# Finishing a job's tokens inside the expert loop of a two-layer transformer kernel, instead of in a pass of its own at the end

## The reference, cut to what matters

```python
def moe_swiglu(t, w_router, w1, w3, w2):          # t: (2048, 1024)
    logits = (t @ w_router).astype(jnp.float32)
    top_v, top_i = lax.top_k(logits, TOP_K)        # 2 of 8 experts
    gates = jax.nn.softmax(top_v, axis=-1).astype(t.dtype)
    e_flat = top_i.reshape(-1)
    order = jnp.argsort(e_flat)
    tok = order // TOP_K
    xs = t[tok]
    sizes = jnp.bincount(e_flat, length=N_EXPERTS).astype(jnp.int32)
    h = jax.nn.silu(lax.ragged_dot(xs, w1, sizes)) * lax.ragged_dot(xs, w3, sizes)
    y = lax.ragged_dot(h, w2, sizes) * gates.reshape(-1)[order][:, None]
    return jnp.zeros_like(t).at[tok].add(y)

# end of the layer: x = x + ga_f * rmsnorm(moe_swiglu(hx), g_ffn_post)
```

## Time and profile before

| | us |
|---|---|
| median of 3 runs | 8557.16 (8553.48 to 8563.33) |
| profiled execution, its own time | 8556.28 |
| its span | 8554.4 |
| TensorE busy | 8155.5 (95%) |
| GpSimd busy | 4284.0 (50%) |
| VectorE busy | 4087.5 (48%) |
| ScalarE busy | 1476.7 (17%) |

### The profile page before, as it was taken

One profiled execution on the slowest core, in us unless ns is written; L12 is line 12 of the kernel. 1 busy time (PEld: TensorE's weight loads), 2 busy tenths in 40 slices (PEclk: granted clock), 3 DMA queues, 4 the chain that ended last, 5 costly groups with the idle time before them and its releaser, 6 DMA issues. The chain is left out here.

```text
span 8554.4 us, 124971 instructions
## 1 busy us (share of the span) xinstructions
PE 8155.5 (95%) x43578; PEld 6035.7 (71%) x43578; DVE 4087.5 (48%) x8920; ACT 1476.7 (17%) x3720; POOL 4284.0 (50%) x4061
## 2 busy tenths in 40 slices
PE   8987999899999999897999999999999999999995
PEld 5575666547777777545777777777777777777774
DVE  3345455334444545644545554455455444444444
ACT  1134323221010101132222111111011011010001
POOL 0010667605656565314666665665665554654433
PEclk9999999999999999998999999999999999999997
DMA  6443788834444443225666666665665555554435
GB/s 262 158 142 121 261 300 298 304 113 170 153 153 158 162 153 106 91 95 183 220 225 228 219 212 214 208 208 196 211 204 194 195 193 177 194 184 161 155 127 199
DMA packets 781420, 1604.46 MB, mean 188 GB/s; under 512 B 47229, under 2 KB 556077, under 8 KB 734465
## 3 DMA queue, kind: packets, MB, share of 16 engines
q1 hardware_dynamic: 735686, 1451.02, 48.3%
q0 software_dynamic: 45280, 147.42, 5.5%
HBM read 1292.61 MB, written 304.71 MB: 187 GB/s over the span
## 5 line engine op out<-in xcount | busy, mean ns | idle before, releaser
L3211 PE MATMUL ex_ps<-ex_xt,ex_w 128*128 x6272 | 956.7, 296 | 31.4 <-issue 31.4
L3211 PEld LDWEIGHTS ex_ps<-ex_xt,ex_w 128*128 128x128 f32 x6272 | 861.3, 191 | 139.7 <-issue 139.7
L3211 PE MATMUL ex_ps<-ex_tx,ex_w 128*128 x6272 | 942.8, 293 | 14.8 <-DVE ex_tmp L3469 14.8
L3522 DVE TENSOR_TENSOR ex_ym<-ex_ps,ex_ym 128x512 f32<-128x512 f32 x1176 | 811.2, 690 | 238.9 <-PE ex_ps L3267 238.8
L3211 PE MATMUL ex_ps<-ex_tx,ex_sm 128*128 x6272 | 887.5, 295 | 15.3 <-issue 12.7
L3211 PEld LDWEIGHTS ex_ps<-ex_tx,ex_w 128*128 128x128 f32 x6272 | 857.5, 191 | 22.9 <-DVE ex_tmp L3469 20.2
L3072 POOL TENSOR_TENSOR ex_sa<-ex_a 128x128 f32<-128x128 f32 x182 | 82.7, 455 | 1561.8 <-DVE ex_a L3461 1561.8
L3211 PEld LDWEIGHTS ex_ps<-ex_tx,ex_sm 128*128 128x128 f32 x6272 | 847.4, 194 | 16.2 <-issue 16.1
L3057 POOL TENSOR_TENSOR ex_sm<-ex_w 128x512 f32<-128x512 f32 x394 | 507.6, 1288 | 119.5 <-DMA ex_w<-in_o_w 74.2
L3329 ACT ACTIVATE ex_tmp<-ex_ps 128x144 f32<-128x144 f32 (+4 forms) x392 | 116.3, 297 | 2350.9 <-PE ex_ps L3211 2350.1
L3063 POOL TENSOR_TENSOR ex_sm<-ex_w,ex_sm 128x512 f32<-128x512 f32 x394 | 501.6, 1273 | 30.9
(11 more groups left out here) (480 smaller groups left out, 14293.2 us busy)
## 6 DMA issues: line engine op xcount, KB each, us to landing
ex_w<-in_o_w SPq DMA_DIRECT2D x593, 1024.0 KB, 5.0
ex_wt<-wt SPq DMA_DIRECT2D x197, 1024.0 KB, 7.0
ma_cqT<-in_o_w SPq DMA_DIRECT2D x112, 1024.0 KB, 7.2
wt<-ma_bt SPq DMA_DIRECT2D x112, 1024.0 KB, 5.1
de_wr<-in_e_w SPq DMA_DIRECT2D x88, 1024.0 KB, 5.3
xs<-de_zero POOLq DMA_DIRECT2D x136, 512.0 KB, 4.8
en_ch<-in_w_mod SPq DMA_DIRECT2D x48, 1024.0 KB, 5.5
de_w<-in_e_w SPq DMA_DIRECT2D x44, 1024.0 KB, 7.3
```

The costliest lines, as they stand in the source:

```text
L3211: last = nc.tensor.matmul(PS[:, bank, 0:h], left[:, k], right[k], start=start and k == 0, stop=k == HK - 1, skip_group_check=not start)
L3522: nc.vector.tensor_tensor(out, new, out, ALU.add).then_inc(y_added[t], 1)
```

## The change

- `finish` handles 4 tiles (512 table rows, those of the last job) instead of 16. It gathers `z` and `x` by GpSimd (8 indirect DMAs) through an index array `LAST`, and each scatter to `out` waits for the one before.
- While a job runs, the tokens of the job before are finished: 4 tiles of 128 rows, in two buffers `Z`. GpSimd gathers the `z` rows after steps 0 (tiles 0, 1), 6 and 7. ScalarE squares and sums them and takes the roots (`roots`, after chunks 1 and 8), followed by a small Silu (`warm`); VectorE inverts (`invert`, after chunks 2 and 9); ScalarE scales (`norms`, after chunks 3 and 10); GpSimd multiplies by the gate's row and issues a gather of `x` that adds into the tile (`scale`, after steps 4, 5, 11, 12), and scatters to `out` (`store`, after steps 5, 6, 12 and ahead of step 13). A token is stored once for each of its two jobs, and the later store is the whole one.
- ScalarE's loop over chunks 0 to 9 becomes a loop over 0, 1, then chunks 2, 3, a loop over 4 to 8, and chunk 9.
- SyncE no longer waits for `stored` at a job's front; the loads of `IX` are issued between chunk 10's and chunk 11's weight loads. `y_free` is gone: VectorE and GpSimd wait for `stored` themselves. At the job's end SyncE waits for the stores to `out` and loads `LAST`.

The diff, cut to its core:

```diff
-def finish(nc, z_d, x_d, order_d, gate, out):
-    DEPTH = 8
+def finish(nc, z_d, x_d, LAST, gate, out):
+    TILES = LAST.shape[1]
...
         @block.gpsimd
         def _(pool):
-            pool.wait_ge(const_in, 32)
-            for t in range(NT):
+            for t in range(TILES):
+                pool.indirect_dma_start(out=Z[:, t], out_offset=None, in_=z_d, ...).then_inc(z_in[t], 16)
+            for t in range(TILES):
+                pool.indirect_dma_start(out=X[:, t], out_offset=None, in_=x_d, ...).then_inc(x_in[t], 16)
+            for t in range(TILES):
                 pool.wait_ge(summed, t + 1)
+                if t:
+                    pool.wait_ge(stored, 16 * t)
                 pool.indirect_dma_start(out=out, ...)
...
@@ SyncE in experts
                     load_low(e, 1, 1)
-                    row = listed(sp, 0, j, ROWS_END)
-                    sp.wait_ge(stored, j * 64 + 64)
-                    sp.sem_inc(y_free, 1)
+                    sp.wait_ge(tr_done, j * (2 * TILES) + 2 * TILES)
+                    load_x(sp.snap((j + 1).with_bounds(min_val=1, max_val=JOBS)))
+                    replace(0, 0, e, 2, None, None)
+                    with sp.Fori(0, (FC - 4) // 2) as q: ...
+                    sp.wait_ge(stored, j * 64 + 64)
+                    row = listed(sp, 0, j, ROWS_END)
...
                     sp.wait_ge(y_added[t], i * job + (job + 1))
+                    sp.wait_ge(o_stored[0], j * 32 + 32)
+                    sp.wait_ge(o_stored[1], j * 32 + 32)
+                    sp.dma_start(LAST[:, :, :], names(0, BANK)[:, 14:16].rearrange("(t p) w -> p t w", p=P)).then_inc(last_in, 16)
@@ GpSimd in experts
+            def gather(j, tile):
+                s = tile % 2
+                if tile == 0:
+                    pool.wait_ge(last_in, j * 16 + 16)
+                    pool.wait_ge(stored, j * 64 + 64)
+                if tile >= 2:
+                    pool.wait_ge(o_stored[s], j * 32 + 16)
+                pool.indirect_dma_start(out=Z[:, s], out_offset=None, in_=z_d, ...).then_inc(z_in[s], 16)
+            def scale(j, tile):
+                s = tile % 2
+                pool.wait_ge(normed, j * 4 + (tile + 1))
+                nc.gpsimd.tensor_tensor(Z[:, s], Z[:, s], G[:, :], ALU.mult).then_inc(scaled, 1)
+                pool.wait_ge(scaled, j * 4 + (tile + 1))
+                pool.indirect_dma_start(out=Z[:, s], out_offset=None, in_=x_d, ..., compute_op=ALU.add).then_inc(x_added[s], 16)
+            def store(j, tile):
+                s = tile % 2
+                pool.wait_ge(x_added[s], j * 32 + 16 * (tile // 2 + 1))
+                if tile:
+                    pool.wait_ge(o_stored[1 - s], j * 32 + 16 * ((tile - 1) // 2 + 1))
+                pool.indirect_dma_start(out=out, ..., in_=Z[:, s], in_offset=None).then_inc(o_stored[s], 16)
...
                     for f in range(FC):
+                        if f == FC - 1:
+                            store(j, 3)
                         step(f, 1 - f % 2, j * (FC // 2) + (f + 1) // 2)
+                        if f == 0:
+                            gather(j, 0)
+                            gather(j, 1)
+                        if f in (4, 5, FC - 3, FC - 2):
+                            scale(j, {4: 0, 5: 1, FC - 3: 2, FC - 2: 3}[f])
+                        if f in (5, 6, FC - 2):
+                            store(j, {5: 0, 6: 1, FC - 2: 2}[f])
+                        if f in (6, 7):
+                            gather(j, f - 4)
                         if f == FC - 2:
                             gather_gates(j, h)
                     add_rows(i, j, t, h)
@@ ScalarE in experts
+                    def roots(pair):
+                        for s in range(2):
+                            tile = 2 * pair + s
+                            act.wait_ge(z_in[s], j * 32 + 16 * (pair + 1))
+                            nc.scalar.activation(XT[:, bass.ds(other, 1), HK:HK + 2, :]..., Z[:, s], ACT.Square,
+                                                 accum_out=ss[:, 0, tile:tile + 1]).then_inc(squared, 1)
+                        nc.scalar.activation(ss[:, 1, 2 * pair:2 * pair + 2], ss[:, 0, 2 * pair:2 * pair + 2], ACT.Sqrt, ...).then_inc(rooted, 1)
+                        nc.scalar.activation(warm[:, :], eps[:, :], ACT.Silu)
+                    def norms(pair):
+                        act.wait_ge(inverted, j * 2 + (pair + 1))
+                        for s in range(2):
+                            nc.scalar.activation(Z[:, s], Z[:, s], ACT.Copy, scale=ss[:, 2, 2 * pair + s:2 * pair + s + 1]).then_inc(normed, 1)
-                    with act.Fori(0, FC - 4) as f:
+                    with act.Fori(0, 2) as f:
                         chunk(f)
+                    roots(0)
+                    chunk(2)
+                    chunk(3)
+                    norms(0)
+                    with act.Fori(4, 9) as f:
+                        chunk(f)
+                    roots(1)
+                    chunk(9)
                     for f in range(FC - 4, FC):
                         chunk(f, TURNS.get(f, ()))
+                        if f == FC - 4:
+                            norms(1)
@@ VectorE in experts
-                            dve.wait_ge(y_free, j + 2)
+                            dve.wait_ge(stored, j * 64 + 64)
...
-                    chunk(0)
-                    chunk(1)
-                    with dve.Fori(2, FC - 4) as f:
+                    for f in range(3):
                         chunk(f)
+                    invert(0)
+                    with dve.Fori(3, 9) as f:
+                        chunk(f)
+                    chunk(9)
+                    invert(1)
```

More of the change, by code:

```diff
@@ L2834, in _ @@
             act.wait_ge(eps_set, 1)
-            for t in range(NT):
-                act.wait_ge(z_in[t % DEPTH], 16 * (t // DEPTH + 1))
+            for t in range(TILES):
+                act.wait_ge(z_in[t], 16)
                 if t:
                     act.wait_ge(squared, t)
-                nc.scalar.activation(junk[:, :], Z[:, t % DEPTH], ACT.Square, accum_out=stat[:, 0, t:t + 1]).then_inc(squared, 1)
+                nc.scalar.activation(junk[:, :], Z[:, t], ACT.Square, accum_out=stat[:, 0, t:t + 1]).then_inc(squared, 1)
                 act.wait_ge(squared, t + 1)
@@ L2845, in _ @@
             nc.vector.memset(eps[:, :], EPS).then_inc(eps_set, 1)
-            dve.wait_ge(const_in, 32)
-            for t in range(NT):
-                s = t % DEPTH
+            dve.wait_ge(const_in, 16)
+            for t in range(TILES):
                 dve.wait_ge(rooted, t + 1)
@@ L2851, in _, with experts @@
                 dve.wait_ge(inverted, t + 1)
[L2852 removed]
+                nc.vector.scalar_tensor_tensor(Z[:, t], Z[:, t], stat[:, 2, t:t + 1], G[:, :], ALU.mult, ALU.mult).then_inc(scaled, 1)
                 dve.wait_ge(scaled, t + 1)
[L2854 to L2858 removed]
+                dve.wait_ge(x_in[t], 16)
+                nc.vector.tensor_tensor(X[:, t], X[:, t], Z[:, t], ALU.add).then_inc(summed, 1)
+def experts(nc, xs_d, cols, ident_d, w1, w3, w2, wt, CT, GG, tab_d, no_share_d, share_d, z_d, x_d, gate, out, LAST):
     F = w1.shape[2]
@@ L2972, in _ @@
                     load_low(e, 0, 0)
+            sp.dma_start(G[:, :], gate.rearrange("(a n) -> a n", a=1).to_broadcast([P, D])).then_inc(g_in, 16)
+            sp.dma_start(LAST[:, :, :], table[ROWS_END:ROWS_END + BANK, 14:16].rearrange("(t p) w -> p t w", p=P)).then_inc(last_in, 16)
             sp.dma_start(share_d[SEQ:SEQ + BANK], no_share_d).then_inc(shares_in, 16)
@@ L3023, in _ @@
                         sp.sem_inc(ix_in, 16 * (7 - small))
-                    sp.wait_ge(tr_done, j * (2 * TILES) + 2 * TILES)
-                    sp.sem_inc(passed_sp, 1)
-                    load_x(sp.snap((j + 1).with_bounds(min_val=1, max_val=JOBS)))
-                    replace(0, 0, e, 2, None, None)
-                    with sp.Fori(0, (FC - 4) // 2) as q:
-                        for s in range(2):
-                            f = q * 2 + (s + 1)
-                            replace(f, 1 - s, e, at(f + 2), e, at(f + 1))
                     replace(FC - 3, 1, e, FC - 1, e, FC - 2)
@@ L3045, in _ @@
             sp.wait_ge(sums["s4"], (n + ahead) * (2 * FC) + 2)
+            sp.sem_inc(passed_sp, 1)
+            sp.wait_ge(last_in, (n + ahead) * 16 + 16)
             sp.sem_inc(passed_sp, 1)
@@ L3145, in _ @@
             weight_sums(1, 0, 1, 0)
+            pool.wait_ge(g_in, 16)
             for t, h in enumerate(HALVES):
@@ L3568, in build @@
         POS = m.sbuf("pos", [P, 2, NT], U32)
+        LAST = m.sbuf("last", [P, BANK // P, 2], U32)
         CT, GG = m.sbuf("ct", [1, 4, LIST], I32), m.sbuf("gg", [P, 3, NT])
@@ L3577, in build @@
                     a["blank"], a["names"], table, POS, CT, RI, GG, ident)
-        experts(nc, xs, cols[1, 1, :, 0], ident, a["o_w1"], a["o_w3"], a["o_w2"], wt, CT, GG, table, a["no_share"], share, z)
```

(3 more changed lines are left out.)

95 lines of the change are left out of this document (62 added, 33 removed).

## The result

The changed kernel takes 8628.45 us (median of 4 runs, 8625.57 to 8630.5) beside 8557.08 us before: ratio 1.0082, 95% interval 1.0071 to 1.0094. It is slower by 71 us where 19 were forecast, and the time lies above the range.

The account below looks back on a forecast made before the run. GpSimd was taken to set the time at job fronts, TensorE in the expert stage, with DMA work bare in `finish`. 58 + 12 + 7 - 39 - 19 = +19 gave 8576 us, 8-in-10 range 8540 to 8612.

Parts of the forecast that it names:

- Costed at nothing: Expert stage: other steps' GpSimd work (at most 5.8 us) fits its idle time ahead of `left_sums`, 8.6 us in the mean chunk.
- Finish: Tail after the experts: fewer tiles end it at 8515 instead of 8554.4 us, gain 39 us, between 31 and 46.
- The bounds for a store's landing: In `finish`: each of four successive stores takes between 3.95 and 7.65 us; 5.5 was taken.
- the stretch before it: From the last L3136 to the barrier ahead of `finish`: claimed to stay as it was.
- Table loads: ScalarE, h = 128 jobs: only the loop over chunks 0 and 1 still reloads for `keep`; gain 19 us.
- Fronts and clock: Job fronts: GpSimd's added `scale` and `store` delay TensorE, 58 us; seven new gaps lower its clock, 12 us.
- Norms: ScalarE, second pair's `norms` between `take` and `keep`: `keep` 2.0 us late, costing TensorE 7 us in all.
- Rival 1: Job fronts: GpSimd's new work does not reach TensorE, so the 58 and 12 us vanish, 8506 us; chance 12%.
- Rival 2: GpSimd waits for landings at 11 fronts, 22 us, and `roots` for `z` in h = 128 jobs, 8; 8601 us; 20%.
- Rival 3: ScalarE's table loads stay where they are, so 19 us of gain are missing, 8595 us; chance 10%.
- VectorE's inversions, SyncE's move and the DMA traffic: Expert stage: two inversions, earlier loads at the front and some 6 MB more DMA in a job, all put at no cost.

## Why the prediction was wrong

The sign was right, and the size was 52 us short. The step that failed is in **Costed at nothing**: "The other steps' GpSimd work [...] lies in GpSimd's idle time ahead of `left_sums`". The cover was taken as a mean over all chunks, and only GpSimd's own lateness was asked about. The work behind step 11 does lie in that idle time (7.12 us of it are left in the rows above), and still it costs 39.5 us: it holds VectorE, whose token sums of chunks 12 and 13 run beside it, and TensorE waits for VectorE. The work behind step 12 was costed, but for its delay of GpSimd at the front alone; it holds VectorE's token sums of chunk 13 too, another 15.2 us. Together they are the +54.7 us of the table above. This is shown by the product and its gather moved one chunk on their own (-37 us), the product and the adding gather left out one at a time (23.2 and 32.3 us left), the lone product at two places (14 and 0 us), and the work moved away altogether. What the adding gather adds is less clear: it holds VectorE only together with a weight sum behind it, and how the two do that stays open. No rival had this mechanism either, though it could be read in the trace of before. There VectorE's timeline in chunk 12 of job 5 has

```profile
5672.92 0.85 DVE L3408 TENSOR_TENSOR ex_tx<-ex_xt  x1
...
5674.30 0.38 DVE L3415 TENSOR_TENSOR ex_tx<-ex_xt  x1
```

and GpSimd's last weight sum there ends between the two:

```profile
5672.23 1.29 POOL L3063 TENSOR_TENSOR ex_sm<-ex_w,ex_sm 128x512 f32<-128x512 f32 x1
```

A token sum of the same size takes 0.85 us beside it and 0.38 us behind it. I asked of each new instruction which engine queues behind it, not which instruction of another engine runs at its time.

The other steps:

- **Finish** (-39): -40.7. The bounds for a store's landing held; ScalarE's first square started 6.2 us behind the barrier's end and the first store 13.7 us behind it, where 11 had been taken; the stores 4.1 to 5.1 us apart made up for that. That the stretch before it stays was wrong by 4.3 us: the barrier's wait grew from 10.1 to 14.4 us. Why was not tried.
- **Table loads** (-19): the mechanism right, 8 loads left as said. Chunks 3 to 9 gave 16.7; chunk 2, which was to give 2.4, cost 2.8, mostly in job 0, whose `roots` waits for `z` (+4.1 us there). Sum -13.9.
- **Fronts and clock** (+58 and +12): 55.4. Behind h = 128 24.6 us came for 27, behind h = 144 16.9 for 22 and 8 of clock, behind the first two h = 160 jobs 14.2 for 9 and 3. Taken apart, TensorE stands 36.7 us longer where 58 were forecast, and its products take 18.5 us more where the clock was to cost 12. The clock term had nothing behind h = 128, because the clock fell there already; but the gaps are now split between chunks 0 and 1, it falls in both, and the products there take 7.3 us more. Why the standing time came out 21 us short of the sum stays open. That GpSimd's order sets the front is shown: without product 36.0, without adding gather 40.9, with all of it moved ahead of chunk 12 -2.2.
- **Norms** (+7): +4.3, in chunks 10 and 11, and 0.0 when `norms(1)` no longer follows a `take`.
- **Rival 1** (the work doesn't reach TensorE) is dead by the fronts. **Rival 2** (landings) is small: the last store's gap is 1.1 to 1.6 us in the h = 128 and h = 160 jobs where 0.30 is usual, and 0.3 to 0.5 in the h = 144 jobs, 6.5 us more over the 11 fronts where 22 were put; and job 0's `roots` waits for `z`. It ends nearest the measured time, but by another cause. **Rival 3** (loads stay) is refuted by the count of 8.
- VectorE's inversions, SyncE's move and the DMA traffic: in the version with everything ahead of chunk 12, chunks 3 to 9 gave 16.7, as with the Silu alone, and chunks 10 and 11 cost 0.0. These leave no room in chunks 3 to 11 for a price above 1 us.
- Slips in the sums, none of which the miss hangs on: with 6.4 us a front the lower bound of the fronts is 52 us and not 48; Rival 2's terms, 22 and 8, add up to 30 where 25 were put in; and the norms at 1 us in four jobs and 0.5 in ten are 9 us and not 7.

The prices of the parts are then +55 fronts, +55 chunks 12 and 13, +4 norms, -14 loads, -41 finish, +4 barrier, and +8 ahead of the experts, whose cause stays open: +71.

## What to carry to other kernels

Before work is put into an engine's idle time, look at what the other engine does in that stretch: the same 2.4 us product cost 0 us a job behind step 8 and 1.1 behind step 11. The two engines' timelines have to be read together wherever VectorE works from SBUF alone. And when a transfer is moved earlier on one engine, check the whole ring of waits: a consumer one chunk earlier than its gather allows cost 16 us a job, and the place that was best for the finished tokens (8516 us) lay one step away from the worst (8752 us).

## What the runs showed of the hardware

- A VectorE sum with both operands in SBUF (0.37 us for its tile) stood until GpSimd's running operation was over: 1.68 and 2.05 us beside a 2.35 us product. Beside back-to-back 128x512 weight sums it took 0.85 us. Additions with one operand in PSUM stayed at 0.68 us in all of these.
- An adding indirect DMA on GpSimd (1.57 us) with a weight sum behind it held the same sum for 2.19 and 2.77 us, and a plain store (1.00 us) with a weight sum behind it for 2.17 us, each until 0.25 us behind the weight sum's end. An adding DMA with no weight sum behind it did not: token sums took 0.38 us beside it.
- TensorE's granted clock was 0.57 in the 4 us behind a gap of 2.94 us, 0.52 behind one of 2.89 us, and 1.00 behind one of 0.65 us.
- Behind the 128x1024 product GpSimd stood 0.79 us ahead of its adding gather, where 0.15 had been assumed and 0.30 is usual between two DMAs.
- One Silu ahead of ScalarE's loops removed all 40 table loads of `keep` (-17 us in chunks 3 to 9).
